# A first layer that multiplies its raw input: the row roots are applied to the projections' results, and the input arrives already turned

## The reference

```python
def rms_norm(x, g):
    y = xf * lax.rsqrt(jnp.mean(xf * xf, axis=-1, keepdims=True) + EPS)
    return (y * g).astype(x.dtype)

def even_layer(h, mem, ...):
    u = rms_norm(h, norm_g)
    proj = u @ w_in                       # 1024 x 7168
    aq, ak, av, az, bh, bc, bb, bz, xq, xz = split(proj)
    ya = differential_attention(aq, ak, av, ...)      # q and k normalised per head
    yb = bb * causal_depthwise_conv(bc * bh, w, b)    # width 512, 3 taps along the tokens
    yx = memory_cross_attention(xq, mem, ...)
    y = concat([ya * silu(az), yb * silu(bz), yx * silu(xz)])
    return h + y @ w_out
```

## Time and profile before

| what | value |
|---|---|
| median of 3 runs | 907.5 us (906.45 to 907.53) |
| profiled execution, its own time | 906.51 us |
| its span in the profile | 904.7 us |
| PE busy | 886.0 us, 98% |
| PEld busy | 742.3 us, 82% |
| DVE busy | 691.9 us, 76% |
| ACT busy | 512.3 us, 57% |
| POOL busy | 86.1 us, 10% |
| DMA | 177.69 MB, mean 196 GB/s |
| PE in the chain that ended last | 89% of the span |
| first matmul of the first layer | 11.18 us from the span's start |

### The profile page before, as it was taken

How to read it: one execution, slowest core, us unless ns; L and a number is a source line. 1 busy time by engine, 2 the same in 40 slices (tenths; PEclk the granted TensorE clock), 3 DMA queues, 4 the chain that set the end, 5 groups by cost and what they waited for, 6 DMA issues and landing times.

```text
span 904.7 us, 13741 instructions
## 1 busy us (share of the span) xinstructions
PE 886.0 (98%) x5040; PEld 742.3 (82%) x5040; DVE 691.9 (76%) x1086; ACT 512.3 (57%) x902; POOL 86.1 (10%) x82
## 2 busy tenths in 40 slices
PE   6999999999999999999999999999999999999997
PEld 5878788999788888989889887877777688888885
DVE  6789989779776668888898765978747779877553
ACT  6567656664445555555667547456644755555441
POOL 0303121100000101012211100100000100010000
PEclk9999999999999999999999999999999999999999
DMA  9855644737574757678767764553224568866641
GB/s 331 277 186 190 217 152 155 242 117 253 199 275 146 228 160 236 235 248 287 236 232 245 236 209 129 164 170 97 93 73 145 158 196 267 288 204 186 194 156 46
DMA packets 103123, 177.69 MB, mean 196 GB/s; under 512 B 7117, under 2 KB 32146, under 8 KB 102930
## 3 DMA queue, kind: packets, MB, share of 16 engines
q1 hardware_dynamic: 99856, 167.27, 56.5%
q0 software_dynamic: 2896, 9.42, 3.1%
q10 hardware_dynamic: 306, 0.14, 0.1%
HBM read 175.71 MB, written 1.07 MB: 195 GB/s over the span
## 4 chain that ended last, share of the span: by engine, by line
PE 89%; DVE 5%; ACT 3%; issue 1%; POOL 1%; DMA 0%; ACTq 0%; DVEq 0%; POOLq 0%
PE acc L1298 17%; PE acc L1300 17%; PE acc L1299 17%; PE acc L1360 9%; PE acc L1361 4%; PE acc L1309 4%; PE acc L1311 4%; PE acc L1310 4%; DVE wlo L2143 2%; PE tp L1455 1%; PE spsum L1439 1%; PE opsum L1578 1%; PE spsum L1442 1%; POOL small L2741 1%; PE tp L1423 1%
## 5 line engine op out<-in xcount | busy, mean ns | idle before, releaser
L2143 DVE TENSOR_TENSOR wlo<-raw,whi 128x1024 fp32r<-128x1024 f32 (+2 forms) x274 | 323.8, 1189 | 100.0 <-ACT whi L1703 99.3
L1703 ACT CAST whi<-raw 128x1024 fp32r<-128x1024 f32 (+2 forms) x274 | 278.0, 1026 | 110.0 <-PE acc L1300 67.9
L1298 PE MATMUL acc<-whi,xx 128*128 128x512 f32 (+1 forms) x384 | 156.1, 407 | 2.2 <-DVE xx L2668 1.0
L1300 PE MATMUL acc<-whi,xx 128*128 128x512 f32 (+1 forms) x384 | 148.8, 388 | 0.0
L1299 PE MATMUL acc<-wlo,xx 128*128 128x512 f32 (+1 forms) x384 | 148.1, 386 | 0.0
L1360 PE MATMUL acc<-xx,whi 128*128 128x512 f32 x352 | 125.1, 400 | 0.8 <-DVE xx L2653 0.8
L1361 PE MATMUL acc<-xx,wlo 128*128 128x256 f32 x352 | 98.8, 281 | 0.0
L1309 PE MATMUL acc<-xx,whi 128*128 128x256 f32 x320 | 94.0, 294 | 0.0
L2741 POOL TENSOR_TENSOR small<-small,half_neg 128x8 f32<-128x8 f32 (+4 forms) x30 | 50.5, 1683 | 446.2 <-DVE small L2104 270.5
L1311 PE MATMUL acc<-xx,whi 128*128 128x256 f32 x320 | 90.5, 283 | 0.0
L1310 PE MATMUL acc<-xx,wlo 128*128 128x256 f32 x320 | 90.5, 283 | 0.0
(11 more groups left out here) (409 smaller groups left out, 1392.5 us busy)
## 6 DMA issues: line engine op xcount, KB each, us to landing
raw<-in_e_w_in SPq DMA_DIRECT2D x56, 512.0 KB, 5.6
raw<-in_o_w_in SPq DMA_DIRECT2D x56, 512.0 KB, 5.7
raw<-in_w_mod SPq DMA_DIRECT2D x48, 512.0 KB, 4.4
raw<-in_w_ffn_in SPq DMA_DIRECT2D x44, 512.0 KB, 4.9
raw<-in_w_in SPq DMA_DIRECT2D x28, 512.0 KB, 3.8
raw<-in_w_ffn_out SPq DMA_DIRECT2D x22, 512.0 KB, 4.3
raw<-in_e_w_out SPq DMA_DIRECT2D x16, 512.0 KB, 6.5
raw<-in_o_w_out SPq DMA_DIRECT2D x16, 512.0 KB, 5.3
```

Of the source, the lines that this page charges most:

```text
L1298: mm(o, hi, whi[:, slot, k, 0:pan.ncols], start=a, stop=False)
L1300: last = mm(o, lo, whi[:, slot, k, 0:pan.ncols], start=False, stop=z)
L1703: nc.scalar.copy(slab(whi, s.i % SPLIT_SLOTS, 0, s.nk, n), slab(raw, s.raw.i % RAW_SLOTS, s.koff, s.nk, n)).then_inc(S["hi_ready"], 1)
L2143: tt(slab(wlo, slot, 0, s.nk, n), slab(raw, s.raw.i % RAW_SLOTS, s.koff, s.nk, n), slab(whi, slot, 0, s.nk, n).bitcast(F32), ALU.subtract) ...
```

## The change

In the first layer the rows of `x` are no longer normalised ahead of the product.

- The host hands over `x` turned as well (`x_t`, in the layout of `mem_t`) and the small vectors already turned (`vec_cols`). SP loads slab 0, a quarter of `x_t` (256 KB, into `g1`), slab 1, the next quarter, and so on to slab 3; then slab 4, half of `x`, slab 5, the other half. ACT makes the high part of `xx` straight from `x_t` with the gain as scale, DVE the low part (`x_part`); the 16 transposes and the two of the vectors are gone. At the very start DVE clears part of `pbuf`, and PE multiplies it five times (`warm_first`).
- The squares of `x` and its root (`fold_stat`, `x_rstd`) are made behind sub 2, `setup_gains` behind sub 4 in place of sub 0, the turned memory's load is issued behind sub 5 in place of sub 2.
- Behind the product: `evac_norm` puts the row's scaled epsilon in place of the constant one; `evac_copy` and the `tok` gates work in two halves of 128 tokens with the root (or half of it) as scale; DVE multiplies a head's own root with the row's. In the `col` panels the tokens lie along the free axis, so the 256 roots must stand in every partition: POOL writes them to DRAM (`row_out`, behind sub 16) and reads them back into all partitions (`row_in`, behind sub 22) as `x_row`, in `negcum`. DVE then multiplies five accumulators by it: in place ahead of the gate of the cross attention, `conv_c` and `conv_z` (`gate_scale`), and out to `g2` for `conv_h` and `conv_b`, where ACT's two copies go.
- `conv` comes behind sub 67 in place of sub 63. The two last `gate_add` steps, of chunks 10 and 11 in the third layer, come one sub later.

```diff
@@ class Plan @@
-                 "gate": ("tanh_ready", "gate_ready"), "conv_h": ("v_evac",), "conv_c": ("conv_u",),
-                 "conv_b": ("v_evac",), "conv_z": ("tanh_ready", "gate_ready"),
+                 "gate": ("tanh_ready", "gate_ready"), "conv_h": ("conv_ev",), "conv_c": ("conv_u",),
+                 "conv_b": ("conv_ev",), "conv_z": ("tanh_ready", "gate_ready"),
...
+                    if pan.w == "e_w_in" and ev.kind in ("evac_conv_c", "evac_conv_z") or ev.kind == "evac_gate" and ev.tile == 12 and pan.w == "e_w_in":
+                        self.tick(ev, "row_scaled")
+                        self.steps.append(Step("gate_scale", first=ev))
                     self.steps.append(ev)
...
-            self.at(self.pos + 2, lambda: self.tick(self.step("gate_add", chunk=chunk, first=st), "gate_sb"), 2)
+            self.at(self.pos + (2 if chunk < 6 else 3), lambda: self.tick(self.step("gate_add", chunk=chunk, first=st), "gate_sb"), 2)
@@ make_plan @@
-    stat = pl.row_stat(0, "g0", ("loaded_x0", 16))
-    first = pl.row_scale(stat, "g0", dve=(0, 1), act=())
-    stat = pl.row_stat(1, "g0", ("loaded_x1", 16))
-    pl.step("setup")
-    second = pl.row_scale(stat, "g0", dve=(0, 1), act=())
-    pl.step("pull")
-    pl.transposed_by_k("g0", (first, second), "x", ROW["e_norm"], None, pull=(3,))
-    pl.at(2, lambda: pl.step("load_mem_t"))
-    pl.at(0, lambda: pl.step("setup_gains"))
+    pl.step("warm_first", q=5)
+    for k in range(KT):
+        if k % 2 == 0:
+            pl.step("pull")
+        pl.tick(pl.step("x_part", scale=ROW["e_norm"], q=k), "rt_hi", "rt_lo")
+    pl.src["x"] = pl.count["rt_lo"], KT
+    pl.fresh = 4
+    pl.at(2, lambda: pl.step("pull"))
+    pl.at(2, lambda: pl.rows_stat("x", "g0", ("loaded_x0", "loaded_x1")), 1)
+    pl.at(5, lambda: pl.step("load_mem_t"))
+    pl.at(16, lambda: pl.step("row_out"))
+    pl.at(22, lambda: pl.step("row_in"))
+    pl.at(4, lambda: pl.step("setup"), -1)
+    pl.at(4, lambda: pl.step("setup_gains"))
...
-    st = pl.step("conv", gate=ev.on["gate_ready"])
-    pl.tick(st, "ytmp_ready", "yhi_ready", "y_ready")
...
+    def conv_out():
+        st = pl.step("conv", gate=ev.on["gate_ready"])
+        pl.tick(st, "ytmp_ready", "yhi_ready", "y_ready")
+        for k in range(8, 12):
+            pl.tile_ready[k] = st.on["y_ready"]
+    pl.at(pl.pos + 3, conv_out, 1)
@@ SP @@
-            for t in range(NT):
-                sp.dma_start(rows_of["g0"][:, t, :], w["x"][0, t * P:(t + 1) * P, :]).then_inc(S[f"loaded_x{t}"], 16)
...
-                if r.i == 2:
+                if r.i < 4:
+                    sp.dma_start(x_t[:, 2 * r.i:2 * r.i + 2, :], w["x_t"][:, 2 * r.i * T:(2 * r.i + 2) * T].rearrange(
+                        "p (k t) -> p k t", t=T)).then_inc(S[f"loaded_xt{r.i}"], 16)
+                else:
+                    t = r.i - 4
+                    if t < NT:
+                        sp.dma_start(rows_of["g0"][:, t, :], w["x"][0, t * P:(t + 1) * P, :]).then_inc(S[f"loaded_x{t}"], 16)
+                if r.i == 5:
@@ PE @@
+            def warm_first(st):
+                pe.wait_ge(S["warm_in"], 1)
+                for _ in range(st.q):
+                    mm(acc[:, 0, 0:3 * P], pbuf[:, 0:P], pbuf[:, 0:3 * P], start=True, stop=True)
@@ ACT @@
+            def x_part(st):
+                k = st.q
+                act.wait_ge(S["loaded_cols"], 16)
+                act.wait_ge(S[f"loaded_xt{k // 2}"], 16)
+                f(xhi[:, k, :], x_t[:, k, :], ACT.Copy, scale=scale_cols(st.scale)[:, k:k + 1]).then_inc(S["rt_hi"], 1)
...
+                if "row_scaled" in st.on:
+                    wait(("row_scaled", st.on["row_scaled"]))
+                f(gates[:, st.tile:st.tile + n, :], acct(st.acc, n), ACT.Tanh, scale=0.5).then_inc(S["tanh_ready"], 1)
@@ DVE @@
+            def x_part(st):
+                k = st.q
+                wait(("rt_hi", st.on["rt_hi"]))
+                stt(xlo[:, k, :], x_t[:, k, :], scale_cols(st.scale)[:, k:k + 1], xhi[:, k, :].bitcast(F32), ALU.mult,
+                    ALU.subtract).then_inc(S["rt_lo"], 1)
+
+            def gate_scale(st):
+                ev = st.first
+                dve.wait_ge(S["sub_done"], ev.done)
+                wait(("row_in", 16))
+                z = acct(ev.acc)
+                tt(z, z, by_row(z), ALU.mult).then_inc(S["row_scaled"], 1)
+
+            def evac_conv_hb(st):
+                dve.wait_ge(S["sub_done"], st.done)
+                wait(("row_in", 16))
+                at = 0 if st.kind == "evac_conv_h" else 1024
+                z = acct(st.acc)
+                tt(g2[:, at:at + 1024].rearrange("p (c t) -> p c t", t=T), z, by_row(z), ALU.mult).then_inc(S["conv_ev"], 1)
...
@@ pv_late (DVE) @@
+                link(tt(stat(st, 2)[:, 0:NT], stat(st, 2)[:, 0:NT], x_rstd, ALU.mult))
@@ POOL @@
+            def row_out(st):
+                wait(("rstd_ready", pl.fold_rstd["x"]))
+                for t in range(NT):
+                    pool.dma_start(row_scratch[t * P:(t + 1) * P, :], x_rstd[:, t:t + 1]).then_inc(S["row_out"], 16)
+
+            def row_in(st):
+                wait(("row_out", 16 * NT))
+                pool.dma_start(x_row, row_scratch.rearrange("t o -> o t").to_broadcast([P, T])).then_inc(S["row_in"], 16)
```

More of the change, by code:

```diff
@@ L160, in __init__ @@
         self.src = {}
+        self.fold_rstd = {}
         self.tile_ready = {}
@@ L210, in panel @@
                  "mix": ("sq_ready", "sq_ready", "v_evac", "v_evac"), "end": (), "ffa": ("ff_lo", "ff_sum", "tanh_ready", "gate_ready"), "ffb": ("ff_lo", "ff_sum", "ytmp_ready", "yhi_ready", "y_ready")}
-        frees = {"norm": "qk_evac", "copy": "v_evac", "gate": "gate_ready", "conv_h": "v_evac", "conv_c": "conv_u",
-                 "conv_b": "v_evac", "conv_z": "gate_ready", "resid": "resid_done", "forget": "forget_sb",
+        frees = {"norm": "qk_evac", "copy": "v_evac", "gate": "gate_ready", "conv_h": "conv_ev", "conv_c": "conv_u",
+                 "conv_b": "conv_ev", "conv_z": "gate_ready", "resid": "resid_done", "forget": "forget_sb",
                  "rope": "rope_done", "normrope": "norm_mid", "ctxkv": "norm_mid", "latkv": "norm_mid",
@@ L334, in transposed, with rows_stat @@
         return after
-    def memory_stat(self):
-        st = self.step("mem_stat")
+    def rows_stat(self, which, src, loaded):
+        st = self.step("fold_stat", which=which, src=src, waits=loaded)
         self.tick(st, "sq_ready", "ms_ready", "rstd_ready")
         self.uses(st, "scr", "sq_ready")
-        self.mem_rstd = st.on["rstd_ready"]
+        self.fold_rstd[which] = st.on["rstd_ready"]
     def memory_parts(self, scale, pos):
@@ L729, in make_plan @@
     pl.memory_parts(ROW["o_mem"], [b - 8, b - 7, b - 4, b - 3])(lambda: pl.load("x", rows_lo=pl.count["rt_lo"]))
-    pl.panel(W, 4608, CW, "x", "conv_c", "col", h_evac=ch.on["v_evac"])
+    pl.panel(W, 4608, CW, "x", "conv_c", "col", h_evac=ch.on["conv_ev"])
     for k in range(3):
@@ L986, in retention @@
     return lambda: ret_out(1)
-PASSABLE = ("sub", "split", "load_mem", "load_mem_t", "mem_stat", "mem_part", "rows_T", "evac_norm", "evac_copy", "evac_gate", "evac_conv_h", "evac_conv_c", "evac_conv_b",
+PASSABLE = ("sub", "split", "load_mem", "load_mem_t", "fold_stat", "mem_part", "gate_scale", "setup", "row_out", "row_in", "setup_gains", "rows_T", "evac_norm", "evac_copy", "evac_gate", "evac_conv_h", "evac_conv_c", "evac_conv_b",
             "evac_conv_z", "qkT", "scores", "PT", "pv", "oT", "forget_rows", "mod", "mod_out", "mod_take", "mod_row", "mod_turn", "gate_rows", "gate_spread", "gate_add", "load", "g_q", "gqa_kT", "g_scores", "g_exps", "g_norm", "g_PT", "g_pv", "ret_arg", "ret_exp", "ret_two", "kfb", "forget_turn", "rope_tables", "mod_cols", "conv_taps", "conv_mul", "conv", "evac_ffa", "evac_ffb")
@@ L1847, in evac_copy @@
                     wait(("gate_sb", 2))
-                if st.panel.w in memory_panels:
-                    wait(("rstd_ready", pl.mem_rstd))
+                if st.panel.w in fold_of:
+                    which = fold_of[st.panel.w]
+                    wait(("rstd_ready", pl.fold_rstd[which]))
                     for t in range(NT):
-                        last = f(grp(*st.dst)[:, t * CW:t * CW + CW], acc2(st.acc)[:, t, :], ACT.Copy, scale=mem_rstd[:, t:t + 1])
+                        last = f(grp(*st.dst)[:, t * CW:t * CW + CW], acc2(st.acc)[:, t, :], ACT.Copy,
+                                 scale=folds[which][1][:, t:t + 1])
                     last.then_inc(S["v_evac"], 1)
@@ L2849 @@
     w_out = named["w_out_2"]
-    named["mem_t"] = np.ascontiguousarray(named["mem"][0].T.reshape(KT, P, T).transpose(1, 0, 2).reshape(P, KT * T))
+    for name, a in (("mem_t", named["mem"]), ("x_t", named["x"])):
+        named[name] = np.ascontiguousarray(a[0].T.reshape(KT, P, T).transpose(1, 0, 2).reshape(P, KT * T))
+    named["vec_cols"] = np.ascontiguousarray(named["vec_rows"][0:P + 9, :].T)
```

98 lines of the change are left out of this document (47 added, 51 removed).

## The result

| what | before | changed kernel |
|---|---|---|
| median of 5 runs, one chip | 906.45 us (905.78 to 907.53) | 911.89 us (910.43 to 912.33) |
| ratio, 95% interval | | 1.0056 [1.0046, 1.0067] |
| profiled execution: own time, span | 906.51, 904.7 us | 911.89, 910.1 us |
| PE busy | 886.0 us | 891.0 us |
| first product of sub 0 / 8 / 12 | 11.18 / 33.12 / 43.99 us | 7.95 / 33.18 / 45.79 us |

The forecast was 907.6 with a range to 910.8. The last two lines of the table say where the time came from. At sub 0 the changed kernel is 3.2 us ahead; at sub 12 it is 1.8 behind; until sub 62 nothing more happens; from there to sub 72 another 3.0 us are lost; behind it, little. So the loss has two places. The first, subs 7 to 12, costs 4.8 us, of which the lead of 3.0 that was left at sub 6 pays for a part; the second, subs 63 to 72, costs 3.0.

The account below looks back on a forecast made before the run. The prediction took PE as the bound, busy 886.0 of 904.7 us. It summed -3.4 (start), +0.9 (subs 7 and 8) and +2.6 (scalings, subs 60 to 71) to +0.1, 907.6 us at the median, range 904.6 to 910.8.

Follow-up runs that it names:

- gains10: Changed kernel with `setup_gains` alone moved from behind sub 4 to behind sub 10: 909.51 us, ratio 1.0027.
- conv0: Changed kernel with `conv` put back behind sub 63: 913.89 us, ratio 1.0080.
- fill: Changed kernel with one short matmul without use ahead of sub 7 and two ahead of sub 8: 909.14 us, ratio 1.0030.
- sqmid: Changed kernel with the squares of `x` moved ahead of the cast of sub 6: 907.87 us, ratio 1.0014.
- pull67: Changed kernel with the cast and `wlo` of sub 67 put between `gate_scale` and the convolution's gate: 909.51 us, ratio 1.0032.
- best1: Changed kernel with squares of `x` ahead of sub 6's cast, `setup_gains` behind sub 10, sub 67's cast ahead of the gate: 905.11 us, ratio 0.9982.
- best2: The kernel of best1 with `conv` one sub earlier, behind sub 66: 904.10 us, ratio 0.9969.
- after2: The changed kernel unaltered, run once more beside fill2 on one chip: 909.66 us, ratio 1.0032.
- fill2: The same kernel as fill, run on another chip beside after2: 908.91 us, ratio 1.0029.
- noscale: Changed kernel with the moves of gains10 and sqmid, without the row-root product ahead of the convolution's gate (result differs): 904.62 us, ratio 0.9977.
- best3: The kernel of best2 with the cast and `wlo` of sub 63 ahead of `conv_b`'s product: 902.40 us, ratio 0.9956.
- nowarm: The kernel of best2 without the five matmuls at the very start: 905.11 us, ratio 0.9985.

## What to carry to other kernels

When the start of a pipeline is moved ahead, follow every resource that the pipeline returns to, not just its inputs: here PE would have come to sub 8 at 30.2, `wlo` was ready at 32.0 (29.6 in gains10), and the accumulator only at 33.1, because its release runs through a root that takes 3.8 us on POOL. A step that waits for a late load must not stand in front of work that is ready: moving 2 us of squares over one such cast won 4.2 us by sub 12 in the profiled executions (41.60 against 45.79), 1.7 of them the clock's, which not every execution loses. And price a pause of PE with what the clock may take behind it, at each pause that the forecast itself contains.

## What I had not expected of the hardware

- Pauses of about a microsecond and then 1.8 us, 3 us apart, can bring PE to half rate for 3.4 us, in some executions of one kernel and not in others. Of the four traces with these pauses three have the fall; conv0's profiled execution had pauses of 1.18 and 1.86 us at the same places and kept its clock there, and then lost it behind 4.36 us. Three matmuls on zeros in the pauses were enough to keep it in both profiled executions. What decides between a fall and none stays open.
- The traces lie in two groups for a reason that is far from the change. In the third layer a pair of matmuls takes 0.353 us in the profiled execution of the kernel before (14 pairs from 767.74 to 772.68) and 0.346 in that of fill (14 pairs from 767.74 to 772.59). Each of the fourteen traces has one of the two: 0.353 the kernel before, the changed kernel, gains10, sqmid, pull67, best1 and best2; 0.346 to 0.347 after2, fill, fill2, conv0, noscale, best3 and nowarm. The changed kernel is in both. From sub 200 to sub 273 that is 217.5 us against 215.6. What decides it stays open. The pair of profiled executions in the table at the top lies in one group, so its 5.4 us are free of this; for a comparison of one microsecond the trace at a fixed sub ahead of that stretch says more than the median.
